# Attention of a hybrid layer: q_hi in both row halves against K_hi over K_lo, V_hi beside V_lo, K and V split once before the loop

## What is computed

```python
SEQ, N_Q_HEADS, N_KV_HEADS, HEAD_DIM, WINDOW, BLOCK = 1024, 16, 4, 64, 128, 128

def sliding_window_attention(q, k, v, sinks):
    nb = s // BLOCK                                   # 8 blocks of 128 queries
    g = N_Q_HEADS // N_KV_HEADS                       # 4 query heads for one kv head
    kb, vb = band(k), band(v)                         # the block before and this one: 256 keys
    scores = einsum('bnqhgd,bnkhd->bnhgqk', qb, kb) * HEAD_DIM ** -0.5
    scores = where(valid, scores, NEG_INF)
    m = maximum(max(scores), sink)
    p = exp(scores - m)
    p = p / (sum(p) + exp(sink - m))
    return einsum('bnhgqk,bnkhd->bnqhgd', p, vb)

q = rms_norm(q.reshape(b, s, N_Q_HEADS, HEAD_DIM), q_norm_g)
k = rms_norm(k.reshape(b, s, N_KV_HEADS, HEAD_DIM), k_norm_g)
o = sliding_window_attention(q, k, v, sinks) * silu(z_a)
```

## Time and profile before

| | us |
|---|---|
| median of three runs (2641.2 to 2642.66) | 2642.59 |
| span of the profiled execution | 2639.0 |
| first score matmul to the last `weigh` (207 to 687) | 480 |
| PE busy, whole span | 2551.3 (97%) |
| DVE busy, whole span | 1402.0 (53%) |
| ACT busy, whole span | 749.6 (28%) |

### The profile page before, as it was taken

The page is one execution under the profiler, slowest core; times in us unless marked ns, Lnnn a source line. Parts: engine busy times, 40 slices in busy tenths (PEclk is TensorE's granted clock), DMA queues, the critical chain, the costliest instruction groups (busy, mean ns, idle before and its releaser), DMA issues.

```text
span 2639.0 us, 32575 instructions
## 1 busy us (share of the span) xinstructions
PE 2551.3 (97%) x11931; PEld 2096.2 (79%) x11931; DVE 1402.0 (53%) x2180; ACT 749.6 (28%) x1407; POOL 102.1 (4%) x100
## 2 busy tenths in 40 slices
PE   6999999999999999999998899989999999999997
PEld 5868888888788878788786688888888888888886
DVE  6436666666552243345464634474487437743763
ACT  4223333434441121232143232253322112211223
POOL 4000000000000000021000020000100000000000
PEclk8999999999999999999998699999999999999999
DMA  5111111111111121131110012310111111111112
GB/s 170 48 32 49 40 48 40 40 48 40 53 49 49 48 104 48 58 101 52 40 48 24 1 48 64 112 48 25 40 56 48 48 48 48 48 48 48 48 52 76
DMA packets 233403, 140.66 MB, mean 53 GB/s; under 512 B 4382, under 2 KB 228787, under 8 KB 232322
## 3 DMA queue, kind: packets, MB, share of 16 engines
q1 hardware_dynamic: 230258, 125.36, 16.2%
q0 software_dynamic: 3088, 14.54, 1.6%
HBM read 127.30 MB, written 12.58 MB: 53 GB/s over the span
## 4 chain that ended last, share of the span: by engine, by line
PE 91%; DVE 5%; ACT 2%; DMA 1%; issue 1%; SPq 0%; DVEq 0%; ACTq 0%
PE bank L680 27%; PE bank L682 27%; PE bank L681 27%; PE bank L771 1%; PE bank L759 1%; PE bank L732 1%; DVE wlo L1521 1%; PE bank L760 1%; PE bank L761 1%; PE bank L783 1%; PE bank L785 1%; PE bank L784 1%; PE bank L920 1%; PE bank L910 1%; DVE R L1932 0%
## 5 line engine op out<-in xcount | busy, mean ns | idle before, releaser
L680 PE MATMUL bank<-xhi,whi 128*128 128x512 f32 x1088 | 425.4, 391 | 9.6 <-DVE xt L1552 8.4
L681 PE MATMUL bank<-xlo,whi 128*128 128x512 f32 x1088 | 424.3, 390 | 0.0
L682 PE MATMUL bank<-xhi,wlo 128*128 128x512 f32 x1088 | 424.1, 390 | 0.0
L1104 ACT ACTIVATE whi<-wraw 128x1024 fp32r<-128x1024 f32 x158 | 166.8, 1056 | 689.7 <-PE bank L682 689.3
L1521 DVE TENSOR_TENSOR wlo<-wraw,whi 128x1024 fp32r<-128x1024 f32 x217 | 267.7, 1234 | 119.1 <-ACT whi L1104 76.9
L680 PE MATMUL bank<-x4hi,whi 128*128 128x512 f32 x704 | 274.3, 390 | 0.0
L682 PE MATMUL bank<-x4hi,wlo 128*128 128x512 f32 x704 | 273.9, 389 | 0.0
L681 PE MATMUL bank<-x4lo,whi 128*128 128x512 f32 x704 | 273.9, 389 | 0.0
L680 PEld LDWEIGHTS bank<-xhi,whi 128*128 128x128 f32 x1088 | 204.9, 188 | 53.7 <-DVE xt L1552 8.8
L681 PEld LDWEIGHTS bank<-xlo,whi 128*128 128x128 f32 x1088 | 204.8, 188 | 42.8 <-issue 0.2
L682 PEld LDWEIGHTS bank<-xhi,wlo 128*128 128x128 f32 x1088 | 204.8, 188 | 42.8
(11 more groups left out here) (336 smaller groups left out, 4674.0 us busy)
## 6 DMA issues: line engine op xcount, KB each, us to landing
wraw<-in_w_in_dram SPq DMA_DIRECT2D x85, 512.0 KB, 3.8
wraw<-in_ffn_w_up_dram SPq DMA_DIRECT2D x44, 512.0 KB, 3.8
wraw<-in_w_out_dram SPq DMA_DIRECT2D x16, 512.0 KB, 4.1
wraw<-in_xattn_wkv_dram SPq DMA_DIRECT2D x16, 512.0 KB, 3.9
wraw<-in_ffn_w_down_dram SPq DMA_DIRECT2D x16, 512.0 KB, 4.1
xraw<-in_x_dram SPq DMA_DIRECT2D x4, 1024.0 KB, 7.9
x_spill<-xt SPq DMA_DIRECT2D x8, 512.0 KB, 6.3
conv_spill<-tv POOLq DMA_DIRECT2D x8, 512.0 KB, 3.2
```

Source lines behind the costliest of these rows:

```text
L680: pe.matmul(acc, whi[slot][:, k, :], xh, start=(k == 0), stop=False)
L681: pe.matmul(acc, whi[slot][:, k, :], xl, start=False, stop=False)
L682: last = pe.matmul(acc, wlo[slot][:, k, :], xh, start=False, stop=(k == k_tiles - 1))
L1104: act.activation(whi[slot][:, :, :], wraw[slot][:, :, :], ACT.Copy).then_inc(s_whi, 1)
```

## The change

K is normalised in place and rounded once, outside of the loop: for each kv head `kst` holds K_hi in the head's own 64 partitions and K_lo in the other 64. V likewise: `vst` holds for each block and head 64 columns V_hi beside 64 columns V_lo. For each unit ACT copies q, rounded, into both partition halves of `qhd` (two buffers). A score is then one matmul over all 128 rows (q_hi * K_hi + q_hi * K_lo) and one over 64 rows (q_lo * K_hi). `weigh` is two matmuls per key block instead of three, and its result has V_hi's part in one half of the partitions of bank 3 and V_lo's part in the other: ACT copies one half out, and DVE adds the other (`sum_o`); only this releases the bank. The loop over blocks on PE and the loop over q tiles on ACT and DVE are written out. The zero padding is made by ACT instead of GpSimd.

```diff
-                    qh, ql = (w[q:q + 64, gg, hh * P:(hh + 1) * P] for w in (qhi, qlo))
-                    kh, kl = (w[q:q + 64, gg, :] for w in (khi, klo))
-                    pe.matmul(o, qh, kh, start=True, stop=False)
-                    pe.matmul(o, qh, kl, start=False, stop=False)
-                    last = pe.matmul(o, ql, kh, start=False, stop=True)
+                    pe.matmul(o, qhd[u % 2][:, hh * P:(hh + 1) * P], kst[:, g, keys], start=True, stop=False)
+                    last = pe.matmul(o, qlo[q:q + 64, hh * P:(hh + 1) * P], kst[q:q + 64, g, keys],
+                                     start=False, stop=True)
...
                 for kb in range(2):
-                    vh, vl = vhi[:, g // 2, kb, :], vlo[:, g // 2, kb, :]
-                    pe.matmul(ps(3), vh, pthi[:, kb, :], start=(kb == 0), stop=False)
-                    pe.matmul(ps(3), vh, ptlo[:, kb, :], start=False, stop=False)
-                    last = pe.matmul(ps(3), vl, pthi[:, kb, :], start=False, stop=(kb == 1))
+                    pe.matmul(ps(3), vst[:, b + kb, g, :], pthi[:, kb, :], start=(kb == 0), stop=False)
+                    last = pe.matmul(ps(3), vst[:, b + kb, g, :], ptlo[:, kb, :], start=False, stop=(kb == 1))
...
-            pe.wait_ge(s_v, 4)
+            pe.wait_ge(s_klo, 4)
+            pe.wait_ge(s_vlo, 4)
...
+                if n % 2 == 0:
+                    half = n % 4 // 2
+                    act.wait_ge(s_kn, n // 2 + 1)
+                    for p in range(2):
+                        last = act.activation(
+                            kst[64 * p:64 * p + 64, 2 * i + p, P + half * HALF:P + (half + 1) * HALF],
+                            kraw[64 * p:64 * p + 64, i, half * HALF:(half + 1) * HALF], ACT.Copy)
+                    last.then_inc(s_khi, 1)
...
+            act.wait_ge(s_klo, 4)
+            act.wait_ge(s_vt, 1)
+            act.activation(vst[:, 0, :, :], zeros, ACT.Copy, scale=0.0)
...
-                act.activation(qhi[:, gg, :].rearrange("p (h n) -> p h n", h=4), q32[:, gg, :, cur], ACT.Copy)
-                act.activation(khi[:, gg, :], kT32[:, gg, keys], ACT.Copy).then_inc(s_phi, 1)
+                q = 64 * (g % 2)
+                for r in (64 - q, q):
+                    last = act.activation(qhd[g % 2][r:r + 64, :].rearrange("p (h n) -> p h n", h=4),
+                                          q32[q:q + 64, g // 2, :, cur], ACT.Copy)
+                last.then_inc(s_phi, 1)
...
+            for c in range(4):
+                dve.wait_ge(s_v, c + 1)
+                blocks = vst[:, 1 + 2 * c:3 + 2 * c, :, :]
+                dve.tensor_tensor(blocks[:, :, :, DH:P], ps(4 + c).rearrange("p (b g n) -> p b g n", b=2, g=KV),
+                                  blocks[:, :, :, 0:DH].bitcast(F32), ALU.subtract).then_inc(s_vlo, 1)
...
+            def sum_o(u, b, g):
+
+                q = 64 * (g % 2)
+                dve.wait_ge(s_oc, u + 1)
+                o = q32[q:q + 64, g // 2, :, cut(b * P, P)]
+                dve.tensor_tensor(o, ps(3)[q:q + 64, :].rearrange("p (h n) -> p h n", h=4), o, ALU.add)\
+                    .then_inc(s_od, 1)
...
             turned_lo(last_u - 2)
+            sum_o(last_u - 3, NB - 1, 1)
             split(T_Z + 1, (T_Z + 1) % 2)
             turned_lo(last_u - 1)
+            sum_o(last_u - 2, NB - 1, 2)
+            sum_o(last_u - 1, NB - 1, 3)
```

More of the change, by code:

```diff
@@ L202, in hybrid_then_mixer_kernel @@
         sqq = at("sqq", [P, 2, 4, S], F32, E)
-        kT32 = at("kT32", [P, 2, P + S], F32, DD)
-        v32 = at("v32", [P, NB + 1, 2 * P], F32, DD + 9216)
-        rk = at("rk", [P, 2, S], F32, DD + 9216)
+        kst = at("k_stacked", [P, KV, P + S], F32R, DD)
+        vst = at("v_stacked", [P, NB + 1, KV, P], F32R, DD + 18432)
         kraw = at("kraw", [P, 2, S], F32, DD + 18432)
[L207 to L210, removed]
+        rk = [at("rk0", [P, S], F32, DD + 26624), at("rk1", [P, S], F32, TMP + 8 * S)]
         sq16 = at("sq16", [16, S], F32, TMP + 8 * S)
[L212 to L216, removed]
+        Sx = [at(f"Sx{n}", [P, 4, 2 * P], F32, E + 4096 + 4096 * n) for n in range(2)]
+        pthi = at("pthi", [P, 2, 4 * P], F32R, E + 12288)
+        ptlo = at("ptlo", [P, 2, 4 * P], F32R, E + 16384)
+        qhd = [at(f"q_hi_twice{n}", [P, 4 * P], F32R, E + 20480 + 2048 * n) for n in range(2)]
+        qlo = at("qlo", [P, 4 * P], F32R, TMP + 8 * S + 32)
         ohi = at("ohi", [P, KT, S], F32R, DD)
@@ L721, in _ @@
             for n in range(4):
-                pe.matmul(ps(4 + n), head_ones[:, :], rk[:, n // 2, (n % 2) * HALF:(n % 2 + 1) * HALF],
+                pe.matmul(ps(4 + n), head_ones[:, :], rk[n // 2][:, (n % 2) * HALF:(n % 2 + 1) * HALF],
                           start=True, stop=True).then_inc(s_kms, 1)
@@ L771, in turn, with weigh @@
                         last = pe.transpose(ps(6 + kb)[:, hh * P:(hh + 1) * P],
-                                            Sx[par][:, hh, kb * P:(kb + 1) * P], ident[:, :])
+                                            Sx[u % 2][:, hh, kb * P:(kb + 1) * P], ident[:, :])
                 last.then_inc(s_t, 1)
-            def weigh(u, b, g, first=False):
-                pe.wait_ge(s_vlo, 2 * b + (g // 2 + 1))
+            def weigh(u):
+                b, g = u // 4, u % 4
                 pe.wait_ge(s_ptlo, u + 1)
-                if not first:
+                if u:
@@ L800, in _ @@
-            attend(0)
-            with pe.Fori(1, NB) as b:
-                attend(b)
+            for u in range(4 * NB):
+                if u >= 2:
+                    turn(u - 2)
+                if u >= 3:
+                    weigh(u - 3)
+                dense(u + T_CONV, u % 2, xhi, xlo, banks=CONV_BANKS)
+                scores(u)
             last_u = 4 * NB
-            turn(last_u - 2, 0)
-            weigh(last_u - 3, NB - 1, 1)
+            turn(last_u - 2)
+            weigh(last_u - 3)
@@ L807, in _ @@
             dense(T_Z, T_Z % 2, xhi, xlo, banks=CONV_BANKS)
-            turn(last_u - 1, 1)
-            weigh(last_u - 2, NB - 1, 2)
-            weigh(last_u - 1, NB - 1, 3)
+            turn(last_u - 1)
+            weigh(last_u - 2)
+            weigh(last_u - 1)
             pe.wait_ge(s_od, last_u)
@@ L1691, in attend @@
                         turned_lo(u - 2)
+                    if not first_block(b) or g >= 3:
+                        sum_o(u - 3, b if g == 3 else b - 1, (g - 3) % 4)
                     load_rq(b, g, g % 2)
```

136 lines of the change are left out of this document (59 added, 77 removed).

## The result

| | us |
|---|---|
| kernel before, median of four runs | 2641.89 |
| changed kernel, median of four runs (2652.59 to 2656.01) | 2654.16 |
| ratio, 95% interval | 1.0048 (1.0034 to 1.0061) |
| span of the profiled execution, before and after | 2639.0 and 2652.2 |

The change removes six of the eighteen matmuls of the attention's products in each unit (12 + 6 become 8 + 4), and the kernel is 0.5% slower.

A forecast was written before the change was run, and what follows sets the result against it. TensorE's issue was taken to bound the units; +7.5 (units) + 1.5 (ahead) + 1.4 (behind) - 0.2 (dummy activation) = +10.2 us, a span of 2649.2, plus 3.6 from span to median: 2652.8 us. Range 2633 to 2660.

The forecast's parts named there:

- Scores, +0.70 a unit: Score matmuls: eight steps of 0.118 plus seven row switches of 0.195 make 2.31 us instead of 1.61, 0.70 more.
- the GLA pair: Two opposite row switches in the GLA stage, 0.33 to 0.34 us together, read as 0.17 for one switch.
- the cheaper rows: Trace readings of a row switch under 0.195 us, such as 0.13 and 0.15, set aside for shorter loads or fewer columns.
- Weigh, -0.46 a unit: In `weigh`, two of six 128-row matmuls go, with no switch: 2 x 0.232 = 0.46 us less a unit.
- Both together: Score and `weigh` terms in the units: forecast as +0.235 us a unit, x 32 = +7.5 us.
- Ahead of the units, +1.5: Before the first convolution tile, V's zero fill and DVE's four subtractions delay PE by 1.5 us (1.4 to 1.8).
- the lower bounds: Ahead of the units: V's zero fill at 0.51 us, each DVE subtraction 0.60 to 0.69, lowest total 1.4.
- Behind the units, +1.4: After the last unit, two `sum_o` additions make PE wait: +0.6 to +0.69 and +0.69, together +1.4 us.
- DVE and ACT at nothing: In the units, added DVE work (+0.27 us even, about +0.96 odd) and ACT work (under 0.8) fit spare time, costing nothing.
- the granted clock falls: In each unit, alternating rows drop TensorE to 1.2 GHz, 3.3 us lost a unit, 2759 us in all; chance 0.06.
- The faster rival: Row switches between score matmuls cost nothing, so each unit loses 1.126 us: 2609.3 us; chance 0.10.
- the one-direction rival: Only four of the seven score switches cost, 0.11 us more a unit: -8.5, 2634 us; chance 0.06.

The follow-up runs named there:

- e6_before_rows: Kernel before, with the first of each head's three score matmuls taken over 128 rows, giving six more row changes a unit: 2677.11 us, ratio 1.0132.
- e3_weigh6: Changed kernel with two matmuls on V's zero block added to `weigh` in each unit, six as before the change: 2665.06 us.
- e1_pairs: Changed kernel with score matmuls issued in pairs of equal row count, three row changes between them instead of seven: 2628.92 us, ratio 0.9958.
- e4_sum_twice: Changed kernel with the `sum_o` addition done twice on DVE in each unit: 2655.35 us, ratio 1.0054.
- e7_halves: Kernel before, its twelve 64-row score matmuls reordered to alternate between the array's two halves and two banks: 2616.43 us in one run.
- e2_padded: Changed kernel with q_lo zero-padded in two buffers so its score matmul also runs over 128 rows: 2605.55 us, ratio 0.9864.
- e9_before_again: Kernel before, unchanged, run once more for a second look at the granted clock behind the last unit: 2638.96 us.

## Why the prediction was right

The forecast was 2652.8 us, +10.2; measured were 2654.16 and +12.3, in the range and of the forecast sign. From unit to unit 15.14 was forecast and 15.15 measured.

- *Scores, +0.70 a unit.* Measured 2.31 us against 1.61: the sum's own 2.31. The value chosen for a switch, 0.195, was the disputed step, since the GLA pair gave 0.17; the steps after are 0.18 and 0.21 over the normal one. Setting the cheaper rows aside held: e6_before_rows has 0.31 and 0.30 with full loads both ways. That the short identity load is the reason why the step into the transposes is 0.26, here too (404.75 to 405.01), was argued and not tested.
- *Weigh, -0.46 a unit.* Measured 2.32 to 1.86. On the path, as e3_weigh6 shows in its trace.
- *Both together* were to be 32 x 0.70 - 30 x 0.46 = +8.6 from the first dense tile of the stage to the last `turn` (the two last `weigh` come behind it). Measured: 690.20 - 196.94 = 493.26 against 680.58 - 195.97 = 484.61, +8.65.
- *Ahead of the units, +1.5.* From the first thing that ACT does with V to the dense tile: 193.21 to 196.94 is 3.73, before 193.85 to 195.97, 2.12: +1.6. The fill took a step of 0.54 and the subtractions 0.62 each (2.48 / 4), near the lower bounds. The stretch ahead of it was shorter by 0.64, where -0.2 was forecast; but the same code reaches this tile at 193.92 in e1_pairs and at 197.52 in e3_weigh6, so this start says nothing about the change.
- *Behind the units, +1.4.* From the start of ptlo to the dense tile 4.53 against 3.64, and one `weigh` shorter by 0.46 in it: +1.35.
- *DVE and ACT at nothing.* Shortest wait 1.26, over the 1 us that was named; e4_sum_twice shows the cover.
- *What was missed, about 2.7 us*, is the clock behind the last unit. The rival "the granted clock falls" was looked for in the units, where the scores are sparse, and there it stays at 1.00; the term *behind the units* named both waits and their lengths and did not ask what they do to the clock. Up to the z tile the sum's +10.2 stands against a measured +10.06 (697.84 - 687.78); behind it come 3.1 us more, 2.7 of them this clock, which makes the profiled +13.2. The stated range reached 2660 and had room for it, though not on this ground.

The faster rival (no price for a change of rows) and the one-direction rival are refuted by the steps after, 0.30 and 0.33. The page figure behind the first, the Trainium skill's gap of columns / 2.4 + 2.5 ns (TensorE: Matmul & The Clock Gate, Back-to-back issue gap), fits only steps within one number of rows, 0.12 us here. The Trainium skill's rule that changing the mode drains TensorE and changing the tile within it does not (TensorEngine Tiling (Array Packing), Key Properties) is what e6_before_rows and e7_halves show, 0.31 across and 0.115 for a pair in two halves.

What stays open: whether an attention whose two kv heads fill the two halves side by side, as e7_halves does with partners that don't belong together, would beat the padded form. It was not tried.

## What to carry to other kernels

Count the changes of a matmul's row count along TensorE's order before counting matmuls: here six more changes of rows in a unit, 1.17 us, outweighed four score matmuls (0.47) and two `weigh` matmuls (0.46). Grouping them (e1_pairs) turned a loss of 0.5% into a gain of 0.4%, padding with zeros to equal rows (e2_padded) into one of 1.4%. A busy share of 100% does not show them; the distance between ends, and a load that starts when the matmul before it ends, do. Where a change lengthens TensorE's waits, price the clock as well: here up to 2.7 us for two waits longer by 0.6 and 0.7.

## What the runs showed of the hardware that was not expected

- Matmuls of 64 rows in the two halves of the array, into different banks, run side by side: twelve in six steps of 0.115 us (e7_halves), 23 us over the 32 units.
- The same GLA stage, same instructions, takes from 77 us (e6_before_rows, clock 0.78) to 84 us (the changed kernel, 0.69) in these traces. Nor does it take another kernel: from the first L879 to the last L920 the kernel before took 82.8 us in its first trace and 77.5 in its second (e9_before_again). Why was not looked into. For terms of a few microseconds only the landmarks of the stage in question tell. Busy time by stage, the GLA stage of e6_before_rows (window, length, then busy time and instructions of PE, PEld, DVE, ACT and POOL, the granted clock, the DMA share and GB/s):

```profile
1454.00:1531.00 77.00, 68.05 (x449) 50.55 (x449) 54.61 (x73) 28.17 (x50) 0.00 (x0) 0.78 0.03 7
```
